# A two-layer streaming encoder: the end of the projection stage reordered, small copies and stores moved to other places

## What is computed

```
z = x @ w_in                      # columns: q_A | k_A | v_A | c_q | c_kv | k_rope
A: grouped-query attention in a window, 8 heads of 64, 2 key heads, a sink per head, a relative bias
B: latent attention: q = rms(c_q) @ w_uq, split into nope and rope parts; q_lat = q_nope @ w_uk
   scores = q_lat . ckv + rope(q_rope) . rope(k_rope); output = probs @ ckv, then @ w_uv
h = sigmoid(x Wg + bg)[:D] * (yA @ w_proj_a) + sigmoid(x Wg + bg)[D:] * (yB @ w_proj_b)
x = LN(alpha x + h @ w_out);  x = LN(alpha x + ConvGLU(x))
```

## Time and profile before

| what | value |
|---|---|
| median of 3 runs | 1992.0 us (1989.5, 1992.0, 1996.69) |
| the profiled execution, its own time | 1990.17 us |
| its span (first to last instruction) | 1988.4 us |
| mean granted clock of PE | 0.982 |
| PE busy | 1896.4 us, 95% |
| DVE busy | 1023.7 us, 51% |
| ACT busy | 667.6 us, 34% |
| POOL busy | 566.3 us, 28% |
| DMA queue, share of 16 engines | 25.2% |

### The profile page before, as it was taken

The page is one execution under the profiler, slowest core; times in us unless marked ns, Lnnn a source line. Parts: engine busy times, 40 slices in busy tenths (PEclk is TensorE's granted clock), DMA queues, the critical chain, the costliest instruction groups (busy, mean ns, idle before and its releaser), DMA issues.

```text
span 1988.4 us, 32255 instructions
## 1 busy us (share of the span) xinstructions
PE 1896.4 (95%) x12626; PEld 1790.4 (90%) x12626; DVE 1023.7 (51%) x1589; ACT 667.6 (34%) x1372; POOL 566.3 (28%) x252
## 2 busy tenths in 40 slices
PE   7988999999999999999999889999999999999996
PEld 6876788799899999999988778888998999999996
DVE  3457534447764432443664674445587543334447
ACT  2224333442454312332231343334334442123323
POOL 2421111124143234332322211111332432443331
PEclk9999999999999999999989999999999999999998
DMA  6333222242122122221231412323321221222111
GB/s 176 114 87 116 78 81 98 73 151 86 43 85 84 57 70 94 75 69 53 80 119 54 146 42 90 102 78 110 123 79 43 86 78 64 70 97 72 61 59 65
DMA packets 58800, 169.41 MB, mean 85 GB/s; under 512 B 8120, under 2 KB 26216, under 8 KB 50728
## 3 DMA queue, kind: packets, MB, share of 16 engines
q1 hardware_dynamic: 58696, 167.97, 25.2%
HBM read 149.42 MB, written 18.28 MB: 84 GB/s over the span
## 4 chain that ended last, share of the span: by engine, by line
PE 83%; DVE 6%; issue 4%; ACT 2%; DMA 2%; POOL 2%; SPq 1%; POOLq 0%; ACTq 0%; DVEq 0%
PE ps L1429 58%; PE ps L1661 9%; PE ps L1736 3%; PE ps L1459 2%; PE ps L1587 2%; POOL w_lo L617 2%; PE ps L1564 2%; ACT probs L711 1%; PE ps L1634 1%; PE ps L1573 1%; DVE rms L995 1%; DVE probs L1095 1%; DVE st_mx L1066 1%; DVE probs L1065 1%; PE ps L1571 1%
## 5 line engine op out<-in xcount | busy, mean ns | idle before, releaser
L617 POOL TENSOR_TENSOR w_lo<-w_raw,w_hi 128x1024 fp32r<-128x1024 f32 (+3 forms) x248 | 566.1, 2291 | 1387.1 <-ACT w_hi L668 1376.4
L668 ACT ACTIVATE w_hi<-w_raw 128x1024 fp32r<-128x1024 f32 (+3 forms) x244 | 231.2, 968 | 416.5 <-PE ps L1429 398.2
L1429 PE MATMUL ps<-x_hi,w_hi 128*128 128x320 f32 x1504 | 346.1, 311 | 13.3 <-POOL w_lo L617 13.3
L1429 PE MATMUL ps<-x_lo,w_hi 128*128 128x320 f32 x1504 | 345.0, 311 | 0.0
L1429 PE MATMUL ps<-x_hi,w_lo 128*128 128x320 f32 x1504 | 344.8, 311 | 0.0
L1429 PEld LDWEIGHTS ps<-x_hi,w_hi 128*128 128x128 f32 x1504 | 253.6, 189 | 15.0 <-issue 5.9
L1429 PEld LDWEIGHTS ps<-x_lo,w_hi 128*128 128x128 f32 x1504 | 253.9, 189 | 0.0
L1429 PEld LDWEIGHTS ps<-x_hi,w_lo 128*128 128x128 f32 x1504 | 253.6, 189 | 0.0
L1661 PE MATMUL ps<-x_hi,w_hi 128*128 128x320 f32 x512 | 173.8, 339 | 8.5 <-ACT logits L744 8.3
L1334 DVE TENSOR_SCALAR f_conv<-f_ext,vec 128x656 f32<-128x656 f32 x44 | 67.3, 1529 | 211.1 <-ACT tail L879 209.5
L1661 PE MATMUL ps<-x_hi,w_lo 128*128 128x320 f32 x512 | 159.6, 312 | 0.0
(11 more groups left out here) (238 smaller groups left out, 3173.0 us busy)
## 6 DMA issues: line engine op xcount, KB each, us to landing
w_raw<-in_slabs SPq DMA_DIRECT2D x86, 1024.0 KB, 4.8
w_raw<-in_slabs SPq DMA_DIRECT2D x20, 768.0 KB, 4.0
gate_logits<-logits SPq DMA_DIRECT2D x64, 160.0 KB, 1.8
gates<-gate_logits SPq DMA_DIRECT2D x16, 640.0 KB, 6.5
w_raw<-in_slabs SPq DMA_DIRECT2D x16, 640.0 KB, 3.7
ckvc<-in_ckvc SPq DMA_DIRECT2D x16, 256.0 KB, 2.9
ckvc_t<-in_ckvc_t SPq DMA_DIRECT2D x16, 256.0 KB, 3.0
x_in<-in_x_t SPq DMA_DIRECT2D x4, 640.0 KB, 8.7
```

Of the source, the lines that this page charges most:

```text
L617: pool.tensor_tensor(w_lo[:, s % 2, c], w_raw[:, s % 2, c], w_hi[:, s % 2, c].bitcast(F32), ALU.subtract).then_inc(wlo_ready, 1)
L668: A(w_hi[:, s % 2, c], w_raw[:, s % 2, c], ACT.Copy).then_inc(whi_ready, 1)
L1429: ins = MM(out_[:, a, :], w, x[:, t, a * HT:(a + 1) * HT], start=t == 0 and w is wh and x is hi, stop=t == tiles - 1 and w is wl)
```

## The change

- The order of PE's jobs: J_V and the two stream transposes (now J_VN, J_CN) come right behind J_KN, ahead of the queries; J_LAT and J_TOK come between the second and the third rotated job; the fourth rotated job is the last. The unit order of B becomes Bp, Bp, Bs.
- ACT: slab 5 is split ahead of the two square roots, slabs 7 and 8 behind the copies of J_V, slab 9 behind the last rotated job. The streams' rotated queries are packed by ACT (`stream_queries`) instead of DVE. A small exponential stands ahead of slab 9's split. For the units Ap, ACT takes the gates and copies its turned half of unit u+1 before the exponentials of unit u+2, where it stood behind them.
- SP stores keys, values, latents and rotated keys ahead of the rows of `qb`. DVE's peaks no longer wait for stores: peaks(1) waits for the first four rows of `qb` and the packing, take_out(0) for the other four and the stores of keys and values. The waits for the rows move on PE from ahead of scores(0) to the first unit of B.
- PE: scores(0), two gate halves, scores(1), two gate halves, where both scores stood ahead of all four halves.
- Values of a unit As: one product with all 128 rows for the cache and one for the new rows, each 128 columns wide, in place of two of each kind with 64; DVE takes the two diagonal blocks with two copies.
- Places: `w_uk` and `q_nope` lie in `q_lat`, `ukc` in `v_tok`, `q_r` in two parts under `probs` and `y_a`.

The diff, cut to its core:

```diff
-J_WUK, J_KN, J_NOPE, J_ROPE, J_LAT, J_V, J_TOK = 13, 14, 18, 22, 26, 27, 31
+J_WUK, J_KN, J_V, J_VN, J_CN, J_NOPE, J_LAT, J_TOK = 13, 14, 18, 22, 23, 24, 30, 31
+J_ROPE = (28, 29, 32, 33)
...
-        if _k % 2 == 0:
-            UNITS.append(("Bs", _r, 0))
+    UNITS.append(("Bs", _r, 0))
...
+        w_uk = place("w_uk", o, [KVL, 4, P])
+        q_nope = place("q_nope", o + 4 * P, [P, 4, TS])
...
+        ukc = place("ukc", o, [P, 4, KVL])
...
-        q_r = place("q_r", o + 5 * T, [P, 2, T])
+        q_r = [place("q_r0", o + 2 * T, [P, T]), place("q_r1", 0, [P, T])]
...
+                sp.wait_ge(job_taken, layer * NJ + J_VA + 2)
+                settle(sp)
+                sp.dma_start(out["k"][bass.ds(layer, 1)].rearrange("a p n -> p (a n)"), k_t[:, SEQ - WINDOW:]
+                             ).then_inc(kv_stored, 16)
+                sp.dma_start(out["v"][bass.ds(layer, 1)].rearrange("a p n -> p (a n)"), v_t[:, SEQ - WINDOW:]
+                             ).then_inc(kv_stored, 16)
+                sp.dma_start(out["ckv"][bass.ds(layer, 1)].rearrange("a p n -> p (a n)"), ckv_t[:]).then_inc(stored, 16)
+                sp.dma_start(out["kr"][bass.ds(layer, 1)].rearrange("a p n -> p (a n)"), kr_r
+                             ).then_inc(stored, 16)
                 for k in range(2):
                     sp.wait_ge(qr_ready, layer * 2 + k + 1)
                     settle(sp)
                     for q in range(4):
-                        sp.dma_start(qb[NOPE:NOPE + ROPE, 4 * k + q, :], q_r[32 * q:32 * q + 32, k, 0:SEQ]
-                                     ).then_inc(rows_loaded, 16)
-                sp.wait_ge(job_taken, layer * NJ + J_ROPE + 3 + 2)
+                        sp.dma_start(qb[NOPE:NOPE + ROPE, 4 * k + q, :], q_r[k][32 * q:32 * q + 32, 0:SEQ]
+                                     ).then_inc(rotated_loaded[k], 16)
+                sp.wait_ge(job_taken, layer * NJ + J_ROPE[3] + 2)
...
-                sp.dma_start(out["k"][bass.ds(layer, 1)].rearrange("a p n -> p (a n)"), k_t[:, SEQ - WINDOW:]
-                             ).then_inc(stored, 16)
...
+                high(5)
                 for k, (n, width) in enumerate(((J_SCQ, QL), (J_SCKV, KVL))):
                     job(n)
                     A(halves(rms[:, k, :]), pair(n), ACT.Sqrt, bias=RMS_EPS, scale=1.0 / width).then_inc(rms_std, 1)
                 for k in range(KQ):
                     act.wait_ge(cq_scaled, layer * KQ + k + 1)
                     A(cq_hi[:, k, :], cqz[:, k, :], ACT.Copy).then_inc(cq_hi_ready, 1)
-                high(5)
                 high(6)
                 for k in range(4):
                     job(J_KN + k)
                     A(kb[0:NOPE, 2 * k, :], ps[0:NOPE, 2 * ((J_KN + k) % 4), :], ACT.Copy).then_inc(kn_even, 1)
-                for s in range(7, S_GATE + 2):
-                    high(s)
                 for k in range(NB):
                     job(J_V + k)
                     A(v_b[:, k, :], ps[:, 2 * ((J_V + k) % 4), :], ACT.Copy).then_inc(v_b_ready, 1)
+                high(7)
+                high(8)
+                def stream_queries(k):
+                    act.wait_ge(qr_ready, layer * 2 + k + 1)
+                    for q in range(4):
+                        ins = A(q_rs[:, :, 4 * k + q, :],
+                                q_r[k][32 * q:32 * q + 32, SEQ:].rearrange("p (r n) -> p r n", r=NREQ), ACT.Copy)
+                    ins.then_inc(qrs_ready, 1)
+                stream_queries(0)
+                act.wait_ge(sinks_ready, layer * 2 + 2)
+                A(st_es[:, 0, :], nsink_p[:, 0:GH], ACT.Exp).then_inc(exp_table, 1)
+                high(9)
+                stream_queries(1)
...
+                def take_gates(u, steps):
+                    for g in range(NG):
+                        if gate_ends(g)[0] == u and gate_ends(g)[1] in steps:
+                            take_gate(g)
                 take_gate(0)
+                act.wait_ge(exp_table, layer + 1)
                 exps(0)
                 exps(1)
                 take_gate(1)
+                turned_half(0)
                 for u in range(NU):
-                    turned_half(u)
-                    for g in range(NG):
-                        if gate_ends(g) in ((u, 0), (u, 1)):
-                            take_gate(g)
-                    if u + 2 < NU:
+                    if u + 2 < NU and UNITS[u + 2][0] == "Ap":
+                        take_gates(u, (0, 1, 2))
+                        turned_half(u + 1)
                         exps(u + 2)
-                    for g in range(NG):
-                        if gate_ends(g) == (u, 2):
-                            take_gate(g)
+                    else:
+                        take_gates(u, (0, 1))
+                        if u + 2 < NU:
+                            exps(u + 2)
+                        take_gates(u, (2,))
+                        if u + 1 < NU:
+                            turned_half(u + 1)
...
+                for k in range(NB):
+                    dve.wait_ge(v_b_ready, layer * NB + k + 1)
+                    dve.sem_inc(job_taken, 1)
+                take(J_VN, v_new.rearrange("p a n -> p (a n)"), flat(2 * (J_VN % 4), 1024, slice(0, TDEC)))
+                take(J_CN, ckv_new.rearrange("p a n -> p (a n)"), flat(2 * (J_CN % 4), 1024, slice(0, TDEC)))
                 for k in range(4):
                     job(J_NOPE + k)
                     src = pair(J_NOPE + k)
                     dve.tensor_copy(q_nope[:, k, :], src[:, 1, SEQ - HT:]).then_inc(job_taken, 1)
                 for k in range(2):
...
-                    dve.wait_ge(job_taken, layer * NJ + J_ROPE + 2 * k + 3)
-                    link(TT(q_r[:, k, :], cqz[:, 0, :], cqz[:, 1, :], ALU.add))
-                    for q in range(4):
-                        ins = dve.tensor_copy(q_rs[:, :, 4 * k + q, :],
-                                              q_r[32 * q:32 * q + 32, k, SEQ:].rearrange("p (r n) -> p r n", r=NREQ))
-                    ins.then_inc(qr_ready, 1)
...
+                    n0, n1 = J_ROPE[2 * k:2 * k + 2]
+                    job(n0)
+                    TT(halves(cqz[:, 0, :]), pair(n0), halves(cos_t[:]), ALU.mult).then_inc(job_taken, 1)
+                    job(n1)
+                    TT(halves(cqz[:, 1, :]), pair(n1), halves(sin_t[:]), ALU.mult).then_inc(job_taken, 1)
+                    dve.wait_ge(job_taken, layer * NJ + n1 + 2)
+                    TT(q_r[k][:], cqz[:, 0, :], cqz[:, 1, :], ALU.add).then_inc(qr_ready, 1)
+                    dve.wait_ge(qr_ready, layer * 2 + k + 1)
+                    if k == 0:
+                        job(J_LAT)
+                        for hh in range(2):
+                            ins = dve.tensor_copy(
+                                q_lat[:].rearrange("p r (k two n) -> p k two r n", two=2, n=TDEC)[:, :, hh],
+                                ps[:, 2 * (J_LAT % 4) + hh, :].rearrange("p (k r n) -> p k r n", k=4, r=NREQ))
+                        ins.then_inc(job_taken, 1)
+                        take(J_TOK, v_tok[:].rearrange("p a n -> p (a n)"), ps[:, 2 * (J_TOK % 4), :])
+                        dve.wait_ge(bias_loaded, 16 * HEADS + (layer + 1) * 32)
+                        dve.memset(bias_p[0:CHUNK, :, WB - CHUNK:], NEG).then_inc(bias_masked, 1)
+                        dve.memset(bias_p[CHUNK:, :, 0:CHUNK], NEG).then_inc(bias_masked, 1)
...
+                        dve.tensor_copy(y_a[0:HD, :, s0:s0 + TDEC], o[0:HD, 0:HD].rearrange("p (t q) -> p t q", t=GH))
+                        to, src = y_a[HD:P, :, s0:s0 + TDEC], o[HD:P, HD:P].rearrange("p (t q) -> p t q", t=GH)
...
-                dve.wait_ge(bias_loaded, 16 * HEADS + (layer + 1) * 32)
-                dve.memset(bias_p[0:CHUNK, :, WB - CHUNK:], NEG).then_inc(bias_masked, 1)
-                dve.memset(bias_p[CHUNK:, :, 0:CHUNK], NEG).then_inc(bias_masked, 1)
-                dve.wait_ge(stored, layer * (16 * N_STORE) + 16 * (N_STORE - 1))
                 dve.wait_ge(sinks_ready, layer * 2 + 2)
                 dve.wait_ge(bias_masked, layer * 2 + 2)
                 peaks(0)
+                dve.wait_ge(rotated_loaded[0], (layer + 1) * 64)
+                dve.wait_ge(qrs_ready, layer * 2 + 2)
...
+                    if u == 0:
+                        dve.wait_ge(rotated_loaded[1], (layer + 1) * 64)
+                        dve.wait_ge(kv_stored, (layer + 1) * 32)
...
+                for b in range(NB):
+                    start_job(J_V + b)
+                    MM(ps[:, 2 * ((J_V + b) % 4), :], ckv_t[:, b * P:(b + 1) * P], uv[:], start=True, stop=True
+                       ).then_inc(job_done, 1)
+                for n, src in ((J_VN, v_t), (J_CN, ckv_t)):
+                    start_job(n)
+                    for r in range(NREQ):
+                        c = SEQ + r * TDEC
+                        ins = pe.transpose(ps[0:TDEC, 2 * (n % 4) + r // 4, (r % 4) * P:(r % 4 + 1) * P],
+                                           src[:, c:c + TDEC], ident[:])
```

(33 more changed lines are left out.)

71 lines of the change are left out of this document (18 added, 53 removed).

## The result

The changed kernel took **1965.68 us** (median of 4 runs, 1962.86 to 1971.16) against 1991.28 us for the kernel before beside it: a ratio of 0.987, with an interval of 0.9839 to 0.9902. It is 1.3% faster, as forecast in direction, but the forecast was 1951 and its range ended at 1963. Some 15 us of the 41 us expected did not come.

The account below looks back on a forecast made before the run. PE bounds the kernel, with 83% of the chain of waits. Per layer 3.6 + 8.5 + 0 + 3.0 + 5.5 = 20.6, for two 41.2: 1990.2 becomes 1949.0, plus 1.8 for the median, 1951 us; range 1942 to 1963.

Parts of the forecast that it names:

- part B: Tail up to the first turn: PE's idle and low-clock time goes, less a DVE-POOL collision; 8.5 us per layer, ends 5 and 9.8.
- C: Units Ap, ACT taking gates and turned half first: 0 us per layer, ends -3 and +1.9.
- The forecast's own sign of being wrong: Wrong if the cache's wait remains, exponentials' spacing changes in general, or new stretches at clock 0.50 appear.
- A: Slab 5 split ahead of the square roots: 2.1 us idle and 1.5 of low clock go, 3.6 us per layer.
- Rival 1: No DVE-POOL collision in part B or C, and PE's lateness won: 6.4 us more gain, 1945 us; chance 0.20.
- Rival 4: Units Ap: exponentials queue behind turned copies on ACT, 9 us per layer lost, 1969 us; chance 0.06.
- D: Values of units As: 0.66 us instead of 1.03 in each of 8 units, 3.0 us per layer, ends 0 and 3.
- E: First stream cache: PE's wait of 2.35 us and the low clock behind it go, 5.5 us per layer, ends 0 and 5.5.
- Rival 3: Clock falls in the gaps of units Ap, two falls per layer: 6 to 10 us lost, 1959 us; chance 0.12.
- The bound of some 2 us for a pause: A PE pause costs itself and, if it exceeds some 2 us, half of a low-clock stretch behind it.
- Rival 2: First stream cache late again at the first Bs, so E is 0: 1962 us; chance 0.09.
- rival 5: Slab 5's earlier split has no effect because the raw slab or a bank is late: 7.2 us less, 1958; chance 0.04.

Follow-up runs that it names:

- slab-first kernel, experiment 1: The changed kernel with SP issuing gate slab 2 between the first and second four rows of `qb`, ahead of the caches: 1951.55 us, ratio 0.9806.
- the seventh experiment: Slab-first kernel with ACT splitting slab 9 behind the exponentials of units 0 and 1: 1963.78 us, ratio 0.9878.
- the sixth experiment, experiment 6: Slab-first kernel with ACT's old order in all units, exponentials of u+2 before the turned half of u+1: 1948.87 us, ratio 0.9796.
- the fifth experiment: Slab-first kernel with the values of a unit As made by the old products of 64 columns per group: 1960.84 us, ratio 0.9853.
- experiments 4: Slab-first kernel with the units of B in the old order Bp, Bs, Bp: 1971.12 us, ratio 0.9903.
- experiment 12: Slab-first kernel run once more, unchanged: 1952.82 us, ratio 0.9807.

## Why the prediction missed, and where it held

**The step that failed** is the sentence of part B that placed the moved work on ACT and SP: the packings "lie behind splits and before gate 0", the stores "go out while PE makes queries". It asked what the moved instructions cost, but not what the instructions behind them wait for once they come 8 to 10 us sooner. `take_gate(1)` also carries the split of gate slab 2, and that waits for a transfer whose issue moved by 4.1 us where ACT's call for it moved by 12.3. For this wait the sum has no term: B ends at the first turn, and C, the stage behind it, stands at 0. (In both kernels the split of gate 1 precedes the turned half of unit 0, so this is not part C's doing.) No rival covered it: the second looked for a late transfer at the first stream cache only. The price was 8.37 + 5.62 = 14.0 us in two layers against the kernel without the wait, of which 6.3 and 3.7 us are PE's pauses; the rest, 4.0 us, I put down to the low clock and the late units behind them, which was not measured apart. The forecast's own sign of being wrong, new stretches at 0.50, is there at 158 to 162 us.

**A** held: start to keys fell by 3.42 us (3.6 forecast), and undoing it makes that stage 2.3 to 3.2 us longer than in the two traces of the slab-first kernel, and the median of the runs 8.5 us. In the second layer PE's wait of 2.07 us for POOL at slab 5 is gone too, but it lies within the stretch from the output projection to the keys, 696.04 us before and 696.22 after, where the scatter of the clock hides what it was worth.

**B** held but for the wait above: 8.89 and 9.15 us against 8.5. Its collision is there. DVE's second tiny step of the first peaks ran beside POOL's 5.10 us from 140.02:

```profile
141.99 0.81 DVE L1100 SCALAR_TENSOR_TENSOR st_nm<-st_mx,nsink_p 128x4 f32<-128x4 f32 x1
142.84 2.30 DVE L1101 TENSOR_TENSOR st_d<-st_nm,sink_p 128x4 f32<-128x4 f32 x1
```

PE lost 0.81 us by it, where 0.7 was taken, and the seventh experiment got 0.97 back. This also bears out the rule weighed in the prediction, from the Trainium skill, SBUF — State Buffer, Who interferes with whom: a DVE instruction with two SBUF inputs or in a two-port mode and POOL's split exclude each other. These traces agree in seven places, where such a step or group of steps beside POOL's split lasted 0.81 to 7.15 us instead of 0.16 to 1.14, while DVE's peaks out of PSUM kept their 1.22 us. The steps with two inputs among them are the tiny ones. The copies and the normalising steps have one (the copies of the earlier trace rows too, which the prediction put under the clause of two inputs); that they ran in a two-port mode is inferred from the hold, no trace shows the mode. Rival 1 is refuted. (It also counted 1.3 us per layer for a missing collision in B that the sum had priced at 0.7, so it should have read 1946.)

**C** was forecast at 0 with ends of -3 and +1.9. With the slab in time, the stage loses 1.7 and 2.0 us; the sixth experiment puts 1.2 and 1.4 of that down to the new order, with 1.1 given back in the stage behind. The spacing of exponentials is still 6.57 us except at gate 5, where it is 8.41, and there the forecast named the mechanism:

```profile
189.46 2.39 POOL L624 TENSOR_TENSOR w_lo<-w_raw,w_hi 128x1024 fp32r<-128x1024 f32 x1 [12.92 <-ACT w_hi L675]
```

```profile
189.87 2.00 DVE L1100 SCALAR_TENSOR_TENSOR st_nm<-st_mx,nsink_p 128x4 f32<-128x4 f32 x1
```

Rival 4 (exponentials behind turned copies) is refuted by the same spacing.

**D and E** together were forecast at 8.5 us per layer. Their stage became 9.27 and 9.01 shorter, but 1.1 of that is C's (experiment 6), which leaves 8.2 and 7.9. D alone, with E there, is 2.8 (3.0 forecast). E alone, without D, is the fifth experiment against before, 6.5 and 6.2 us, or 5.4 and 5.1 as an estimate with C's 1.1 taken off, and 5.5 were forecast. Taken in this order the two add up. In the other order they do not: D without E brings nothing, and E on top of D is then worth 9.0 to 9.9. In rows, the values of a unit As and what PE does behind them are now 0.73 to 0.83 us apart, 0.66 forecast and 1.02 before. The first product takes 0.42 us in the rows below, where the forecast took a quarter of a row of four, 0.25. That makes 2.0 us per layer of the 2.8; the other 0.8 was not placed:

```profile
210.12 0.49 PE L1667 MATMUL ps<-probs_t,vc 128*128 128x128 f32 x2
210.54 0.48 PE L1668 MATMUL ps<-probs_t,packed 16*128 16x128 f32 x2
210.96 0.42 PE L1697 MATMUL ps<-x_hi,w_hi 128*128 128x320 f32 x1
```

**The sum** of 41.2 us agrees with the slab-first kernel, 1990.17 - 1949.20 = 41.0 us between the profiled executions, 39.5 between the medians (1991.03 - 1951.55). That is in part luck. By stages the 41.0 are 2.5 from start to keys, 18.0 to the first turns (17.0 forecast), -3.7 in the units Ap (0 forecast), 18.3 in As and B (17.0 forecast), and 5.7 in the stretch from the output projection to the keys, where only the second half of A, 3.6 by forecast, has a cause. The 3.7 lost in the units Ap and the 1.1 that the start fell short are made up by 1.0 in B, 1.3 in As and B, and some 2 us of the clock's scatter. **Rival 3** (the clock falls in the gaps of the units Ap) was half right. The pauses are there, and behind gate 5 the clock fell in experiments 4, 5 and 12 and not in the first. But the price was wrong: the stage takes 46.67 us with the fall (experiment 12) and 46.68 without it. DVE and ACT set the pace there: the exponentials stay 6.57 us apart with PE at half its clock, which the forecast's own part C said and the rival's price forgot. The bound of some 2 us for a pause, read from four pauses of the kernel before, does not hold either: the fall at gate 5 came behind two pauses of 1.40 and 1.73 us (experiment 12, up to 184.77 and 187.58 us).

Rival 2 (the cache late again) and rival 5 (A without effect) did not occur: neither wait is there after the change.

## What to carry to other kernels

When a change brings a consumer forward, list for every instruction that moves with it the transfer it waits for, with its issue and its landing time, and move the issue too; a large transfer that is issued ahead is a delay (the slab was there some 11 us after its issue behind the caches, 145.89 to 157.08, and 5.7 us after it ahead of them), and one late transfer holds the next, unrelated instruction in the same engine's program. Price edits that remove waits on the same path together and not one by one: D was worth 2.8 us or nothing depending on E. An edit that gives a wait back one stage later, as C did, has to be taken out before the next stage's gain is booked. To read parts of a few microseconds, compare distances between fixed instructions inside the trace, not whole times.

## What the runs showed of the hardware

- A slab of 1 MB lands in 4.8 us as a median over the program, and in 12.0 us (the median of two) when it is issued behind about 1.9 MB of caches and copies and together with a second slab (the 16 engines were busy for 70% of the stretch from 140 to 160 us). A store of 160 KB behind it took 11.9 us where 1.7 is the median, and 5.9 in the slab-first kernel.
- The clock behind one and the same pause is not reproducible. In a stage that no experiment touches, PE pauses 1.32 us, up to 507.94 us in the trace of after, and 1.31 us, up to 498.92, in that of slab-first. In the 6 us up to 508 and 499 it was busy 3.85 us in either, at a granted clock of 1.00. Rows of after, then of slab-first, the last 2 us before and the first 2 behind:

```profile
506.00:508.00 2.00, 0.68 (x6) 0.45 (x4) 2.00 (x1) 0.52 (x2) 1.80 (x1) 1.00 0.00 0
508.00:510.00 2.00, 2.00 (x8) 2.00 (x9) 2.00 (x6) 1.13 (x2) 0.00 (x0) 0.51 0.42 82
```

```profile
497.00:499.00 2.00, 0.69 (x6) 0.46 (x5) 2.00 (x1) 0.50 (x2) 1.77 (x1) 1.00 0.00 0
499.00:501.00 2.00, 2.00 (x14) 2.00 (x15) 2.00 (x6) 1.13 (x2) 0.00 (x0) 1.00 0.44 90
```

  The stretch from the output projection to the next keys is 690.3 to 696.2 us long in kernels with the same instructions there (mean granted clock 0.99 in the trace with 690.3 and 0.98 in that with 696.2), and that from the second output projection to the end 612.6 to 617.6 us. This is as much as single parts of the change are worth, and about as much as the runs of one kernel differ from each other: 1949.2 to 1955.18 in experiment 1.
- ACT's four packings of 128 columns took 1.27 us beside POOL's split in the first variant as well as alone (141.84 and 134.50 us), while DVE's same four took 5.12 and 0.91. Of the two engines only DVE was held by POOL.
